# Mixture-of-experts stage of a two-block network: experts ordered by list length, and a short-list path that runs two k tiles of the down product side by side

## The reference

```python
D_FF_2 = 2816
N_EXPERTS = 8
TOP_K = 2
...
def swiglu(x, w13, w2):
    gate, up = jnp.split(x @ w13, 2, axis=-1)
    return (jax.nn.silu(gate) * up) @ w2
def moe_ffn(u, w_router, w13, w2):
    ...
    logits = (t @ w_router).astype(jnp.float32)
    top_val, top_idx = lax.top_k(logits, TOP_K)
    top_w = jax.nn.softmax(top_val, axis=-1)
    ...
    for e in range(N_EXPERTS):
        gate_e = jnp.sum(jnp.where(top_idx == e, top_w, 0.0), axis=-1).astype(t.dtype)
        out = out + gate_e[:, None] * swiglu(t, w13[e], w2[e])
```

## Time and profile before

| what | value |
|---|---|
| median of three runs | 3045.09 us |
| profiled execution, its own time | 3047.15 us |
| its span in the profile | 3045.1 us |
| TensorE matmul busy | 2933.4 us (96%) |
| VectorE, ScalarE busy | 1587.7 us, 599.5 us |
| DMA: bytes, mean rate | 733.18 MB, 241 GB/s |
| expert stage (first gather to last scatter) | 2232.8 to 3018.5 us |

### The profile page before, as it was taken

The page is one execution under the profiler, slowest core; times in us unless marked ns, Lnnn a source line. Parts: engine busy times, 40 slices in busy tenths (PEclk is TensorE's granted clock), DMA queues, the critical chain, the costliest instruction groups (busy, mean ns, idle before and its releaser), DMA issues.

```text
span 3045.1 us, 67762 instructions
## 1 busy us (share of the span) xinstructions
PE 2933.4 (96%) x28798; PEld 2587.4 (85%) x28798; DVE 1587.7 (52%) x3012; ACT 599.5 (20%) x1431; POOL 15.6 (1%) x27
## 2 busy tenths in 40 slices
PE   5999999999999999999999989998899999999998
PEld 4999898899999999889999868987786678667875
DVE  7776663277577667326758457889541212111212
ACT  1111114121111111312211311125231111110111
POOL 0000000000000000000000000000000000000000
PEclk8999999999999999999999989999899999999999
DMA  8665655345556565534655527850378998889882
GB/s 317 249 252 192 263 208 201 130 187 204 215 214 260 209 259 222 201 115 162 232 225 201 190 113 281 327 235 26 144 309 336 362 378 348 333 338 382 367 338 106
DMA packets 55545, 733.18 MB, mean 241 GB/s; under 512 B 6609, under 2 KB 6793, under 8 KB 10805
## 3 DMA queue, kind: packets, MB, share of 16 engines
q1 hardware_dynamic: 51364, 716.68, 60.1%
q0 software_dynamic: 3984, 13.74, 1.3%
HBM read 729.31 MB, written 4.23 MB: 241 GB/s over the span
## 4 chain that ended last, share of the span: by engine, by line
PE 88%; DMA 5%; DVE 5%; issue 1%; ACT 1%; SPq 0%; DVEq 0%; ACTq 0%
PE psum L751 35%; PE psum L842 17%; PE psum L1337 14%; PE psum L1381 10%; PE psum L829 3%; DMA ring<-in_up_dram 2%; PE psum L745 2%; PE psum L1397 1%; DMA ring<-in_w_v_dram 1%; DVE ring L1889 1%; DMA ring<-in_w_ccch_dram 1%; PE psum L1362 1%; DMA ring<-in_ada_dram 1%; DMA ring<-in_m_out_dram 1%; PE psum L944 1%
## 5 line engine op out<-in xcount | busy, mean ns | idle before, releaser
L751 PE MATMUL psum<-work,ring 128*128 128x128 f32 x3680 | 440.7, 275 | 2.2 <-ACT work L1471 2.2
L751 PEld LDWEIGHTS psum<-work,ring 128*128 128x128 f32 x3680 | 425.2, 192 | 3.0 <-issue 1.6
L751 PE MATMUL psum<-work 128*128 128x128 f32 x3328 | 390.5, 276 | 3.2 <-DVE work L1983 1.8
L751 PEld LDWEIGHTS psum<-work 128*128 128x128 f32 x3328 | 381.6, 193 | 3.7 <-issue 3.2
L1889 DVE SCALAR_TENSOR_TENSOR ring<-ring,cond 128x1024 f32<-128x1024 f32 x240 | 279.4, 1222 | 83.7 <-DMA ring<-in_ada_dram 83.4
L842 PE MATMUL psum<-work,ring 128*128 128x256 f32 x1344 | 295.6, 382 | 6.9 <-DMA ring<-in_m_out_dram 4.8
L842 PEld LDWEIGHTS psum<-work,ring 128*128 128x128 f32 x1344 | 256.9, 192 | 44.0 <-DMA ring<-in_m_out_dram 5.6
L842 PE MATMUL psum<-h_t,ring 128*128 128x256 f32 x1280 | 278.9, 380 | 1.0 <-ACT h_t L1592 1.0
L842 PEld LDWEIGHTS psum<-h_t,ring 128*128 128x128 f32 x1280 | 242.3, 190 | 36.2 <-issue 3.1
L751 PE MATMUL psum<-h_t,ring 128*128 128x128 f32 x2272 | 266.6, 276 | 4.9 <-DMA ring<-in_up_dram 3.8
L751 PEld LDWEIGHTS psum<-h_t,ring 128*128 128x128 f32 x2272 | 260.0, 192 | 7.7 <-DMA ring<-in_up_dram 5.1
(11 more groups left out here) (381 smaller groups left out, 2912.2 us busy)
## 6 DMA issues: line engine op xcount, KB each, us to landing
ring<-in_ada_dram SPq DMA_DIRECT2D x60, 2048.0 KB, 8.2
ring<-in_up_dram SPq DMA_DIRECT2D x55, 2048.0 KB, 8.6
ring<-in_up_e_dram SPq DMA_DIRECT2D x32, 2048.0 KB, 8.0
work<-in_up_e_dram SPq DMA_DIRECT2D x32, 2048.0 KB, 8.8
ring<-in_down_dram SPq DMA_DIRECT2D x20, 2816.0 KB, 10.6
ring<-in_down_e_dram SPq DMA_DIRECT2D x16, 1792.0 KB, 9.3
work<-in_down_e_dram SPq DMA_DIRECT2D x16, 1792.0 KB, 9.4
ring<-in_w_qk_dram SPq DMA_DIRECT2D x12, 2048.0 KB, 8.5
```

The costliest lines, as they stand in the source:

```text
L751: mm = pe.matmul(bank(bank_of)[:, pair * P:(pair + 1) * P], w, right(i), start=(first and pair == 0 and i == 0), stop=(pair == lin.pairs - ...
```

## The change

VectorE ranks the eight experts by list length with eight-wide max and index instructions and leaves the order in `order`. Expert 0 always comes first (4096 is added to its key), because its weights are on their way before the order is known. A limit of 88 is set for places 0 to 3 of the order, and of 64 for places 4 to 7; `beyond` is zero when every list is within its limit. TensorE then runs `expert(e, 88)` for places 0 to 3 and `expert(e, 64)` for places 4 to 7, and otherwise the loop with 256 columns. With 64 columns up and gather stream 64 columns instead of 88; and down takes even k tiles in column group 0 to 63 and odd ones in 64 to 127, so a bank holds two partial sums, which the scatter adds (its selection has the same ranks in both halves, from `time_twice`). SyncE and VectorE load the expert's number from `order` into a register for each place. The edges of w2's chunks become 0, 8, 14, 22.

```diff
-        "upE": Rounds(2, (4, 4, 3, 4, 4, 3), DT, "up_e"), "downE": Sides((0, 8, 15, 22), "down_e"),
+        "upE": Rounds(2, (4, 4, 3, 4, 4, 3), DT, "up_e"), "downE": Sides((0, 8, 14, 22), "down_e"),
...
                 if "upE" in names:
-                    with sp.Fori(0, times) as e:
-                        stream_rounds(place("upE", e))
-                        stream_sides(place("downE", e))
+                    stream_rounds(place("upE", 0), 0)
+                    stream_sides(place("downE", 0), 0)
+                    sp.wait_ge(signal["ordered"], place("router").of("ordered", 1))
+                    with sp.Fori(1, times) as e:
+                        which = sp.value_load(order[0:1, bass.ds(e, 1)], min_val=0, max_val=NE - 1)
+                        stream_rounds(place("upE", e), which)
+                        stream_sides(place("downE", e), which)
...
-                mm = pe.matmul(psum[0:1, 5 * 512 + S:5 * 512 + S + NE], ones[:, 0:1],
+                mm = pe.matmul(psum[:, 5 * 512 + S:5 * 512 + S + NE], ones[:, :],
...
-                        for n in reversed(range(lists)):
+                        if twice:
+                            for k in range(first, last):
+                                lo = k % 2 * SHORT
+                                mm = pe.matmul(bank(2 * side)[lo:lo + SHORT, :], mid[:, k, 0:SHORT],
+                                               deep_slot[slot][:, (k - first) * 512:(k - first + 1) * 512],
+                                               start=(k < 2), stop=(k >= FT - 2))
+                        for n in () if twice else reversed(range(lists)):
...
-            longest = pe.value_load(count[0:1, 0:1], min_val=0, max_val=S)
-            with pe.If(longest <= NARROW):
-                with hinted_loop(pe, NE) as e:
+            pe.wait_ge(signal["ordered"], place("router").of("ordered", 1))
+            too_long = pe.value_load(beyond[0:1, 0:1], min_val=0, max_val=SHORT * S)
+            with pe.If(too_long <= 0):
+                with hinted_loop(pe, 0, NE // 2) as e:
                     expert(e, NARROW)
+                with hinted_loop(pe, NE // 2, NE) as e:
+                    expert(e, SHORT)
...
-            dve.reduce_max(count[:, :], psum[0:1, 5 * 512 + S:5 * 512 + S + NE], AX).then_inc(dve_done, steps.one())
+            dve.scalar_tensor_tensor(key, psum[:, 5 * 512 + S:5 * 512 + S + NE], float(NE), rank_bias,
+                                     ALU.mult, ALU.add).then_inc(dve_done, steps.one())
...
+            dve.max(ranked, key).then_inc(dve_done, steps.one())
+            dve.wait_ge(dve_done, steps.count())
+            dve.max_index(ranked_at[:, :], ranked, key).then_inc(dve_done, steps.one())
+            tt(margin, ranked, limits, ALU.subtract)
...
+            dve.tensor_copy(order_f[:, 0:NE], ranked_at[:, :]).then_inc(dve_done, steps.one())
+            dve.reduce_max(worst, margin, AX).then_inc(dve_done, steps.one())
+            dve.tensor_copy(time_twice, time).then_inc(dve_done, steps.one())
...
+            dve.tensor_copy(order[:, :], order_f).then_inc(dve_done, steps.one())
+            dve.tensor_scalar(beyond[:, :], worst, 0.0, None, ALU.max).then_inc(dve_done, steps.one())
+            dve.tensor_scalar(shift, worst, 0.0, -float(SHORT), ALU.is_le, ALU.mult).then_inc(dve_done, steps.one())
...
+            dve.tensor_scalar(time_twice[:, SHORT:P], time[:, SHORT:P], shift, None, ALU.add).then_inc(signal["ordered"], 1)
...
+                which = dve.value_load(order[0:1, bass.ds(j, 1)], min_val=0, max_val=NE)
+                dve.tensor_copy(now[:, :], listed[:, bass.ds(which, 1), :].rearrange("p e n -> p (e n)")).then_inc(dve_done, steps.one())
```

More of the change, by code:

```diff
@@ L245, in stages @@
         "glu": Linear(4, 4, 32 * P, "glu"), "ln2": with_(ln_fused, x_last=1),
-        "router": with_(uses(b4=3, b5=1), top=1, ratio=1, gate=1, picked=1),
+        "router": with_(uses(b4=3, b5=1), top=1, ratio=1, gate=1, picked=1, ordered=1),
         "tokens": uses(b0=1, b1=1, b2=1, b3=1),
@@ L348, in loop_on, with hinted_loop @@
     return loop
-def hinted_loop(eng, times):
-    return eng.bass.Fori(0, times, engines=bass.OrderedEngineSet([eng.engine]), hint_back_edge=True)
+def hinted_loop(eng, first, end):
+    return eng.bass.Fori(first, end, engines=bass.OrderedEngineSet([eng.engine]), hint_back_edge=True)
 def at(i, step, k):
@@ L443, in build @@
         now = sb("now", [P, 2 * TT])
-        count = sb("count", [1, 1], I32)
+        beyond = sb("beyond", [P, 1], I32)
+        order = sb("order", [P, NE + 1], I32)
+        ranked_at = sb("ranked_at", [P, NE], U32)
+        rank8 = sb("rank8", [P, 6 * NE + 4])
         def tiles(a, n):
@@ L569, in build @@
                                      gelu_out[32 * i:32 * i + 32, :].rearrange("p (f q b) -> p f q b", f=2, q=4)[:, :, part, :])
-        time = flat(34, 1)
+        time, time_twice = flat(34, 1), flat(35, 1)
+        rank_bias, limits, key, ranked, margin = (rank8[:, n * NE:(n + 1) * NE] for n in range(5))
+        order_f, worst, shift = rank8[:, 40:41 + NE], rank8[:, 49:50], rank8[:, 50:51]
         quarter = small[:, 208:209]
@@ L687, in stream_rounds @@
                     for c, (part, lo, hi) in enumerate(lin.edges):
-                        src = dram[lin.source][p.of("of " + lin.source, part, i, 2)]
+                        src = dram[lin.source][at(i, 2, which * 4 + part)]
                         slot, use = p.deep(c, i)
@@ L1346, in expert @@
                 lists = -(-width // P)
-                slots = lambda n: min(width - n * P, P)
+                twice = width <= SHORT
+                slots = lambda n: P if twice else min(width - n * P, P)
                 p = place("gather", e)
@@ L2997, in _ @@
             scaled(place("ln2"), h, ln_scale)
+            dve.tensor_scalar(rank_bias, iota8[:, :], -1.0, float(NE - 1), ALU.mult, ALU.add).then_inc(dve_done, steps.one())
+            dve.memset(limits[:, 0:NE // 2], float(NE * NARROW + NE - 1)).then_inc(dve_done, steps.one())
+            dve.memset(limits[:, NE // 2:NE], float(NE * SHORT + NE - 1)).then_inc(dve_done, steps.one())
+            dve.memset(order_f[:, NE:NE + 1], float(NE)).then_inc(dve_done, steps.one())
+            dve.wait_ge(signal["gelu_moved"], place("s5").of("gelu_moved", 1))
+            for col in (rank_bias, limits):
+                dve.wait_ge(dve_done, steps.count())
+                dve.tensor_scalar(col[:, 0:1], col[:, 0:1], float(NE * 2 * S), None, ALU.add).then_inc(dve_done, steps.one())
             p = place("router")
@@ L3056, in _, with pick @@
             dve.wait_ge(bank_free[4], reads(p, 4, 2) + 1)
-            def pick(e):
+            def pick(j, places):
                 dve.wait_ge(dve_done, steps.count())
-                dve.tensor_copy(now[:, :], listed[:, e, :]).then_inc(dve_done, steps.one())
+                which = dve.value_load(order[0:1, bass.ds(j, 1)], min_val=0, max_val=NE)
+                dve.tensor_copy(now[:, :], listed[:, bass.ds(which, 1), :].rearrange("p e n -> p (e n)")).then_inc(dve_done, steps.one())
                 dve.wait_ge(dve_done, steps.count())
@@ L3066, in pick @@
                 for t in range(TT):
-                    e_last = dve.tensor_scalar(sel_gate[:, t, :], time, now[:, t:t + 1],
+                    e_last = dve.tensor_scalar(sel_gate[:, t, :], places, now[:, t:t + 1],
                                                now[:, TT + t:TT + t + 1], ALU.is_equal, ALU.mult)
@@ L3072, in pick, with one_expert @@
                 e_last.then_inc(signal["picked"], 1)
-            pick(0)
-            def one_expert(e, between=None):
+            dve.wait_ge(signal["ordered"], place("router").of("ordered", 1))
+            pick(0, time)
+            def one_expert(e, places, between=None):
                 p = place("gather", e)
@@ L3091, in one_expert @@
                         dve.tensor_tensor(mid[:, n, :], mid[:, n, :], half(b), ALU.mult).then_inc(bank_free[b], 1)
-                pick(at(e, 1, 1))
+                pick(at(e, 1, 1), places)
                 p = place("scatter", e)
@@ L3098, in one_expert @@
                                              x[:, f, :], ALU.mult, ALU.add).then_inc(bank_free[b], 1)
-            one_expert(0, x_after)
-            for e in steps.loop("expert", NE - 1):
-                one_expert(at(e, 1, 1))
+            one_expert(0, time, x_after)
+            for e in steps.loop("expert", NE // 2 - 2):
+                one_expert(at(e, 1, 1), time)
+            for e in steps.loop("short expert", NE // 2 + 1):
+                one_expert(at(e, 1, NE // 2 - 1), time_twice)
             layer_norm(place("ln3"))
```

13 lines of the change are left out of this document (9 added, 4 removed).

## The result

The changed kernel takes **2976.28 us** (median of four runs, 2974.48 to 2977.50), the kernel before 3044.47 us on the same chip (four runs, 3039.49 to 3050.99). The ratio is 0.9774, with a 95% interval of 0.9755 to 0.9794. Forecast were 2982 us, so the time lies inside the range. The profiled execution took 2976.49 us, with a span of 2974.4 us, against 3047.15 and 3045.1 before.

What follows compares the result with a forecast made beforehand. TensorE, 96% busy, was taken as the bound, with transfers binding the short experts after the change. Saving 67.4 us less 4.7 added gives 62.7 us: 3047.15 becomes 2984.5, as a median 2982 us; range 2970 to 3003.

Steps and rivals of the forecast that it cites:

- The path and TensorE's work: Places 4 to 7 take the short path; TensorE needs 66.8 us per short expert against 97.7.
- The pairs: Down in places 4 to 7: neighbouring products in different column groups overlap, so down takes 19.0 us.
- the second rival: Down pairs don't overlap: TensorE needs 85.8 us per short expert, 3002 us in all; chance 4%.
- The bound: Short experts are bound by transfers, 84.4 us each against TensorE's 66.8; the last chunk leaves 3.4 us of products.
- The rate: Weight transfers in places 4 to 7 run at 410 GB/s, so 126.9 MB take 309.4 us.
- The start of the second loop: At place 4, a branch stops TensorE for perhaps 2 us once, while the queue goes on; counted at nothing.
- 4.1 + 1.6 + 3.4: Places 4 to 7: us until the queue restarts, lag behind the restart, and products left by the last chunk.
- rows 11: Old trace's first expert: TensorE idle 1.8 of 5 us at clock 1.00, cited against waits lowering the clock.
- Ahead of the first expert: Ordering, register loads and a slower clock before the first gather add 4.7 us.
- the first: Rival: memory gives less over 300 us, 354 GB/s, so transfers take 49 us longer, 3031 us; chance 2%.
- The third: Rival: waits at chunks in places 4 to 7 halve TensorE's clock, about 119 us per expert, 3135 us; chance 5%.
- The fourth: Rival: a list of 64 becomes 65, so all eight experts run with 256 columns, about 4220 us; chance 3%.

Runs made afterwards that it cites:

- the last experiment: Changed kernel with one TensorE loop, 88 columns in gather and up, a branch picking the down product, shared scatter and gather in one piece: 2980.96 us.
- the changed kernel's second measurement: The changed kernel itself, unaltered, measured once more on another chip against the kernel before: 2977.46 us, ratio 0.9785.
- the loop that was too large: Changed kernel with one TensorE loop of about 2038 instructions, gather and up at 88 columns, a branch picking down and scatter code: 3094.91 us.

## Why the prediction was right

The time came out 8.0 us below the forecast for the profiled execution (2976.49 against 2984.5), from steps that were partly wrong. Point by point:

- **The path and TensorE's work: right.** Up products take 29.2 ns each (352 of them in 10.29 us, 2664.14 to 2674.43; forecast 30). Half of the bytes left TensorE's sum bare: 66.6 us, forecast 66.8.
- **The pairs: right.** 88 products in 18.88 us where no chunk is late (the kernel with 88 columns in up) and 19.05 in the last experiment, 215 to 216 ns each; forecast 215, 19.0 us. Without them the period is 85.7 us, which the second rival had at 85.8.
- **The bound: right in kind.** The short experts are bound by the transfers, 1.01 in the DMA share, and the last chunk leaves 3.65 us of products (forecast 3.4).
- **The rate: mis-sized.** The step "34.6 MB at 410 GB/s, the middle of the two long windows" is wrong. Measured are 428 GB/s, which makes 80.9 us and not 84.4, and the 126.9 MB take 296.5 us, 12.9 less than forecast. The window of 405 GB/s held the restart of the queue, with its 2.5 us at 144 GB/s; without them it is 417, and I then charged a lag for the restart once more. That is a part only: the window of 411 GB/s held no restart. In the old kernel the sender also waits for slots. The best stretch there was 424 to 425 GB/s over 12.5 and 20 us:

```profile
2637.50:2650.00 12.50, 12.50 (x336) 12.50 (x333) 0.00 (x0) 4.00 (x11) 0.00 (x0) 1.00 1.01 424
2650.00:2670.00 20.00, 20.00 (x528) 19.89 (x526) 4.22 (x10) 2.30 (x6) 0.00 (x0) 1.00 1.00 407
2670.00:2690.00 20.00, 20.00 (x374) 15.81 (x370) 6.40 (x17) 0.00 (x0) 0.00 (x0) 1.00 1.00 425
```

- **The start of the second loop: missed.** "A branch into the second loop stops TensorE for perhaps 2 us once, while the queue goes on" is the step that failed. TensorE lost 11.9 us in the first round: 7.5 in gaps, some 3.6 because the two pieces behind the long gaps ran at a lower clock (126 products in 5.57 us instead of 3.7 to 3.9, 165 in 6.60 instead of 4.8), and 0.8 in the other pieces. And the queue did not go on as before, since its slots come free by TensorE's products: from 2645 to 2660 us, where the forecast had it at its full rate, it moved 333 GB/s. Of the 315.4 us from the start of up in place 4 to the end of the last down, 18.9 are not transfers at full rate, where I had 9.1 (4.1 + 1.6 + 3.4). That is 9.8 us too little, and it nearly cancels the 12.9 us of the rate: 315.4 measured, 318.5 forecast. The trace of before had shown the effect: rows 11, which I took for a TensorE starved of weights, are the first pass through its own loop, with the same piece of 126 products and no wait for a transfer:

```profile
2257.00 5.07 PE L1337 MATMUL psum<-h_t,work 128*64 128x88 f32 x126 [0.64 <-issue]
2263.88 1.43 PE L1337 MATMUL psum<-h_t,work 128*64 128x88 f32 x30 [1.81 <-issue]
```

- **Ahead of the first expert: right.** The first scatter comes 104.17 us after the transposes of the ranks, 99.71 before: +4.5 us, forecast +4.7. The register load on VectorE shows as 1.05 us of idle time (forecast 1.0):

```profile
2229.26 0.17 DVE L3098 COPY listed<-psum 128x16 f32<-128x16 f32 x1
2230.48 0.17 DVE L3106 COPY now<-listed 128x4 f32 x1 [1.05 <-issue]
```

  and gather at a lower clock takes 4.03 us where it took 2.65; with the transposes that is 1.6 us, forecast 2. The ten instructions cost 1.1 us, forecast 1.7. The last 0.7 us are in up of place 0, whose first pass has gaps of 2.8 us where it had 2.5; no term stood for that.
- **Outside the change: 5 us that were luck.** The expert stage began 2.5 us earlier than in the old trace, from small differences over the 2.2 ms before it. And what follows the last down took 27.5 us instead of 30.1, most of all because the last norm's 16 products took 3.71 us instead of 6.65. The clock in that place varies from run to run, whatever the kernel: 6.64 us with 88 columns in up, 5.37 in the changed kernel's second measurement. Together with the 3.1 us between forecast and measurement from up of place 4 to the last down they are the 8 us.
- **The rivals.** The memory did not give less over 300 us, it gave more: the first fell. The third, the clock, showed its mechanism (0.85 to 0.89 in stretches with waits of 2 to 3 us) but hardly its price: the mean over 232 us was 0.98, and where the transfers are the bound a slower product only shortens the next wait. Its price was paid in the first round of place 4, some 3.6 us, behind gaps that come from the code and not from the weights. The fourth did not come.
- **The marks.** I had written that the forecast is wrong if the last periods differ from 84 us by over 3, or if the clock is under 1.00. Both happened (80.9 us on average; 0.98), and the time was still met. The third mark, stretches at 0 GB/s between short experts, did not: 428 GB/s throughout. The rate itself lay outside the 405 to 418 that I had named. So the marks show what the time hides: 2982 was met by two errors of opposite sign, which is luck in the number, while the path and the bound were right.

*What stays open.* The old wide half shows stretches of 403 to 416 GB/s with a DMA share of 0.98 to 1.01. Two chunks under way give 421 and three 428, so depth may explain a part; what takes the rest there was not tried. How the fetch of code is held up by the weights is not shown either, only that it is by their traffic (22.75 us against 32.7) and not by the depth of their queue. And the stall of 7.8 to 8.7 us at the head of the loop that was too large came with the DMA engines nearly idle; its cause was not tried, beyond that it is absent in the smaller loop.

## What to carry to other kernels

When a step gives an engine time back, ask what the other resource can do at its best, and take that rate from the best stretch (424 to 425 GB/s here), not from a mean over a restart (405); then look for the smallest edit that reaches it, as here the pairs alone do. Count code as a cost: a second version of a loop's body is fetched while the transfers run at full rate, and costs 7 to 12 us in its first pass here; a loop that grows past what the engine holds paid 13 to 20 us in every pass. Share the code of the parts that don't differ. A first pass is in the trace already, as a loop's first turn: read it there.

## What the runs showed of the hardware

- **The fetch of instructions competes with data.** TensorE's new code comes in pieces of 126 products, which are 252 instructions with their weight loads. The instruction queue brings seven packets of 16.4 KB more with the second loop (141 to 148; 142 with one loop), 115 KB, and the loop has some 1812 instructions. With 52 GB/s of other traffic the first 704 products take 22.75 us, with half of the bytes 26.0, with all 32.7, at a pace of 20.8 when the code is there. The Trainium skill (Runtime: NRT & Kernel Launch, "Instruction fetch mechanics") says that an engine's instructions are refilled in blocks of 256, that TensorE's store holds 2048, and that crossing a block's edge is mostly hidden. The pieces of 252 agree with the first. The second is not settled here: a loop of about 1934 stays and one of about 2038 does not, and both are under 2048; an estimate from the page's two figures is that a loop is held in whole blocks, so that 2038 instructions fit in eight blocks of 256 only when they begin within ten of an edge. No run shows where the blocks lie. The last holds at 52 GB/s of other traffic and not beside the full stream of weights. The same section warns that a taken branch outside the window that is held stalls an engine; the loop with 1934 instructions shows no stall, the one with 2038 does, 7.8 to 8.7 us even where the DMA engines move 8 GB/s or less.
- **One core alone moves 428 GB/s** over 232 us, well above the 358 GB/s that the Trainium skill (DMA: Bandwidth & Descriptors, "Where 436 GB/s comes from") gives for a core. The prediction took that figure as it stands; by the same section it is half of what a stack gives its two cores, and no run here has two cores at work.
- **Queue depth.** Two chunks of 2 MB under way: 421 GB/s. Three or more: 428.
